# Decode attention: the row maxima one unit later, the heads' sums over four units, and another sharing of the last batch's value halves

## The reference

```python
def fox_sample(q, k_new, v_new, logf_new, k_past, v_past, logf_past):
    ...
    c = jnp.cumsum(lf_all, axis=1).transpose(0, 2, 1)
    s = jnp.einsum('bqhd,bkhd->bhqk', q, k_all, preferred_element_type=F32) * FOX_SCALE
    s = s + cq[..., :, None] - c[:, :, None, :]
    s = jnp.where(kpos[None, :] <= qpos[:, None], s, -jnp.inf)
    p = jax.nn.softmax(s, axis=-1).astype(v_all.dtype)
    return jnp.einsum('bhqk,bkhd->bqhd', p, v_all)
```

## Time and profile before

| | |
|---|---|
| median of 3 runs | 2482.54 us (2477.68 to 2482.71) |
| the profiled execution | 2480.07 us |
| its span, first to last instruction | 2478.2 us |
| TensorE, VectorE, ScalarE, GpSimd busy | 91%, 38%, 37%, 26% of the span |
| mean granted TensorE clock | 0.951 |

### The profile page before, as it was taken

The page is one execution under the profiler, slowest core; times in us unless marked ns, Lnnn a source line. Parts: engine busy times, 40 slices in busy tenths (PEclk is TensorE's granted clock), DMA queues, the critical chain, the costliest instruction groups (busy, mean ns, idle before and its releaser), DMA issues. The chain is left out here.

```text
span 2478.2 us, 31007 instructions
## 1 busy us (share of the span) xinstructions
PE 2255.6 (91%) x11248; PEld 1820.7 (73%) x11248; DVE 951.0 (38%) x1497; ACT 924.6 (37%) x1455; POOL 648.1 (26%) x390
## 2 busy tenths in 40 slices
PE   6999999889999788999997499699999999995999
PEld 5999999767777566666765278577777888874687
DVE  3334444353663757777776200410021321111000
ACT  4233333223443435777777210422234333333100
POOL 1231121220220001555545542021122111113420
PEclk9999999889999888999998699799999999997999
DMA  6122232201200307899996453432222322214431
GB/s 155 29 54 53 49 82 56 56 23 46 61 14 30 97 1 264 306 319 316 313 312 224 134 153 108 152 105 77 72 92 84 111 71 71 71 37 150 146 102 53
DMA packets 258377, 288.06 MB, mean 116 GB/s; under 512 B 70538, under 2 KB 169740, under 8 KB 258124
## 3 DMA queue, kind: packets, MB, share of 16 engines
q1 hardware_dynamic: 240986, 252.84, 33.0%
q10 hardware_dynamic: 17266, 33.59, 3.7%
HBM read 246.09 MB, written 41.32 MB: 116 GB/s over the span
## 5 line engine op out<-in xcount | busy, mean ns | idle before, releaser
L226 PE MATMUL bank<-whi,x_hi 128*128 128x512 f32 (+1 forms) x1536 | 592.9, 386 | 20.1 <-POOL wlo L206 14.9
L228 PE MATMUL bank<-wlo,x_hi 128*128 128x512 f32 (+1 forms) x1536 | 580.1, 378 | 0.0
L230 PE MATMUL bank<-whi,x_lo 128*128 128x512 f32 (+1 forms) x1536 | 579.5, 377 | 0.0
L226 PEld LDWEIGHTS bank<-whi,x_hi 128*128 128x128 f32 x1536 | 293.0, 191 | 81.9 <-POOL wlo L206 19.4
L230 PEld LDWEIGHTS bank<-whi,x_lo 128*128 128x128 f32 x1536 | 293.1, 191 | 41.6
L259 ACT ACTIVATE projected<-bank 128x512 f32<-128x512 f32 (+1 forms) x160 | 92.1, 576 | 620.6 <-PE bank L230 591.7
L228 PEld LDWEIGHTS bank<-wlo,x_hi 128*128 128x128 f32 x1536 | 293.8, 191 | 39.3 <-issue 0.7
L2069 POOL TENSOR_TENSOR dec_v_lo<-dec_v,dec_v_hi 128x1024 fp32r<-128x1024 f32 x96 | 237.2, 2492 | 220.0 <-ACT dec_v_hi L2417 220.0
L206 POOL TENSOR_TENSOR wlo<-wraw,whi 128x512 fp32r<-128x512 f32 (+1 forms) x192 | 230.5, 1233 | 32.6 <-ACT whi L199 32.6
L2236 DVE TENSOR_TENSOR dec_kt_lo<-bank,dec_kt_hi 128x512 fp32r<-128x512 f32 x256 | 170.4, 684 | 100.6 <-ACT dec_kt_hi L2407 100.2
L2407 ACT ACTIVATE dec_kt_hi<-bank 128x512 fp32r<-128x512 f32 x256 | 150.5, 596 | 107.5 <-PE bank L2096 96.3
(11 more groups left out here) (335 smaller groups left out, 3306.2 us busy)
## 6 DMA issues: line engine op xcount, KB each, us to landing
dec_k<-cache_k SPq DMA_DIRECT2D x256, 256.0 KB, 4.0
dec_v<-cache_v SPq DMA_DIRECT2D x256, 256.0 KB, 4.4
wraw<-w_in_even SPq DMA_DIRECT2D x32, 512.0 KB, 6.4
wraw<-w_in_odd SPq DMA_DIRECT2D x16, 1024.0 KB, 8.5
gv<-projected ACTq DMA_DIRECT2D x4, 2304.0 KB, 8.1
gm_v<-gv SPq DMA_DIRECT2D x8, 1152.0 KB, 6.0
m<-gm_mt ACTq DMA_DIRECT2D x8, 1056.0 KB, 4.1
wraw<-w_in_odd SPq DMA_DIRECT2D x4, 2048.0 KB, 8.8
```

Source lines behind the costliest of these rows:

```text
L226: pe.matmul(bank[:, 0:width], e.xhi[:, k, c:c + P], e.whi[:, k, 0:width], start=(k == 0), stop=False)
L228: pe.matmul(bank[:, 0:width], e.xhi[:, k, c:c + P], e.wlo[:, k, 0:width], start=False, stop=False)
L230: mm = pe.matmul(bank[:, 0:width], e.xlo[:, k, c:c + P], e.whi[:, k, 0:width], start=False, stop=(k == KD - 1))
```

## The change

The row maxima move from unit 36 to 37 of the batch, behind the key split of 36. `heads` is cut in four: the pick of the heads at unit 70 (38 of the next batch), the two sums at 71 and 72, the adding and scaling at 73 (41), each behind its unit's key split. The store of the result goes with `HEADS_AT + 2` from 70 to 75. In the last batch the odd value pieces go to VectorE and the even ones to GpSimd, eight each, where it was four and twelve. `by_vector` and `by_pool`, which count the pieces for the waits, take the batch as well, and SP, GpSimd and TensorE call them with it. The shorter loop bound of TensorE only drops units in which it has nothing to do.

```diff
-HEADS_AT = VALUE_AT[-1] + 2
+MAXES_AT = LOW[-1] + 1
+PICK_AT = VALUE_AT[-1] + 4
+HEADS_AT = PICK_AT + 3
-def on_vector(p):
-    return p % 4 == 3
+def on_vector(r, p):
+    return p % 4 == 3 if r < DB - 1 else p % 2 == 1
...
-                for u in range(UNITS * (DB - 1) + HEADS_AT):
+                for u in range(UNITS * (DB - 1) + VALUE_AT[-1] + 1):
...
-                def heads(r):
-                    s = Chain(steps_t, r)
+                def pick_heads(r):
+                    step_t[0] = Chain(steps_t, r)
                     dve.wait_ge(out_written.sem, out_written.at(r, 2))
                     dve.tensor_tensor(picked_o[:], outb[0:2 * rows, :].rearrange("p (h d) -> p h d", h=H),
                                       own_head[:].unsqueeze(2).broadcast_to([2 * rows, H, HD]), ALU.mult).then_inc(
                         out_read.sem, 1)
+
+                def sum_heads(r, dst, src):
+                    s = step_t[0]
                     dve.wait_ge(out_read.sem, out_read.at(r, 2))
-                    dve.tensor_reduce(o_hi[:], picked_o[0:rows].rearrange("p h d -> p d h"), AX, ALU.add).then_inc(
+                    dve.tensor_reduce(dst[:], picked_o[src].rearrange("p h d -> p d h"), AX, ALU.add).then_inc(
                         s.sem, s.one())
-                    dve.tensor_reduce(o_lo[:], picked_o[rows:2 * rows].rearrange("p h d -> p d h"), AX,
-                                      ALU.add).then_inc(s.sem, s.one())
+
+                def heads(r):
+                    s = step_t[0]
                     dve.wait_ge(s.sem, s.reached())
                     dve.tensor_tensor(o_hi[:], o_hi[:], o_lo[:], ALU.add).then_inc(s.sem, s.one())
...
                             store_scores(r, x)
-                            if x == GROUPS // 2 - 1:
-                                maxes(r)
+                    if rounds_at(u, MAXES_AT) is not None:
+                        maxes(rounds_at(u, MAXES_AT))
                     if n < DB * GROUPS:
                         split_keys(n // GROUPS, n % GROUPS, j)
...
                     for r, p in pieces_at(u, LEAD - 1):
-                        if on_vector(p):
+                        if on_vector(r, p):
                             split_values(r, p)
+                    if rounds_at(u, PICK_AT) is not None:
+                        pick_heads(rounds_at(u, PICK_AT))
+                    if rounds_at(u, PICK_AT + 1) is not None:
+                        sum_heads(rounds_at(u, PICK_AT + 1), o_hi, slice(0, rows))
+                    if rounds_at(u, PICK_AT + 2) is not None:
+                        sum_heads(rounds_at(u, PICK_AT + 2), o_lo, slice(rows, 2 * rows))
                     if rounds_at(u, HEADS_AT) is not None:
                         heads(rounds_at(u, HEADS_AT))
```

More of the change, by code:

```diff
@@ L1840, with by_vector, by_pool @@
 VALUE_AT = [FIRST_VALUE + 3 * p // 2 for p in range(VPIECES)]
-HEADS_AT = VALUE_AT[-1] + 2
-def on_vector(p):
-    return p % 4 == 3
[L1849 to L1856, removed]
+MAXES_AT = LOW[-1] + 1
[3 more added lines that the diff above has]
+    return p % 4 == 3 if r < DB - 1 else p % 2 == 1
+def by_vector(r, p):
+    return sum(on_vector(r, q) for q in range(p + 1))
+def by_pool(r, p):
+    return p + 1 - by_vector(r, p)
 def rounds_at(u, at):
@@ L1979, in attention_block @@
         v_hi_ready = c.begin("v_hi_ready", VPIECES)
-        v_lo_vector = c.begin("v_lo_vector_ready", by_vector(VPIECES - 1))
-        v_lo_pool = c.begin("v_lo_pool_ready", by_pool(VPIECES - 1))
+        v_lo_vector = c.begin("v_lo_vector_ready", by_vector(0, VPIECES - 1))
+        v_lo_pool = c.begin("v_lo_pool_ready", by_pool(0, VPIECES - 1))
         v_used = c.begin("v_pieces_used", VPIECES)
@@ L2037, in load_values @@
                         r, p = (n - RING) // GROUPS, 2 * ((n - RING) % GROUPS) + 1
[L2038 to L2041, removed]
+                        if on_vector(r, p) or on_vector(r, p - 1):
+                            sp.wait_ge(v_lo_vector.sem, v_lo_vector.at(r, by_vector(r, p)))
+                        if not on_vector(r, p) or not on_vector(r, p - 1):
+                            sp.wait_ge(v_lo_pool.sem, v_lo_pool.at(r, by_pool(r, p)))
                     for j, page in pages_of(n):
@@ L2084, in _ @@
                     for p in range(VPIECES):
-                        if not on_vector(p):
+                        if not on_vector(r, p):
                             split_values(r, p)
@@ L2147, in values @@
                         pe.wait_ge(out_read.sem, out_read.at(r, 1))
-                    if on_vector(p):
-                        pe.wait_ge(v_lo_vector.sem, v_lo_vector.at(r, by_vector(p)))
+                    if on_vector(r, p):
+                        pe.wait_ge(v_lo_vector.sem, v_lo_vector.at(r, by_vector(r, p)))
                     else:
-                        pe.wait_ge(v_lo_pool.sem, v_lo_pool.at(r, by_pool(p)))
+                        pe.wait_ge(v_lo_pool.sem, v_lo_pool.at(r, by_pool(r, p)))
                     slot = (VPIECES * r + p) % VRING
@@ L2327, in heads @@
                     s.end()
-                step = [None]
+                step, step_t = [None], [None]
                 def first(dve):
```

## The result

The median of four runs is 2502.97 us (2501.83 to 2505.23), against 2481.89 before (four runs, 2477.68 to 2482.71): a ratio of 1.009, 95% interval 1.0072 to 1.0107, or some 21 us slower. That was the direction forecast, at about twice the forecast size of 10.5. The profiled execution took 2505.23.

What follows compares the result with a forecast made beforehand. TensorE was taken to bound the kernel, busy 47.26 of 51 us. Six boundaries +16.8, first boundary +0.6, last batch -5.5 gave +11.9 us: 2492 to 2494.4 by basis, said as 2493, range 2476 to 2508.

Steps and rivals of the forecast that it cites:

- The walk up to the small sum: VectorE at a middle boundary: exponentials at 3.14 us after the store, small sum due at 10.32, held by GpSimd to 12.02.
- the scaling: VectorE operation after the small sum: taken as not held by GpSimd; the two small operations together take 0.42 us.
- held twice: Rival at the six boundaries: GpSimd holds small sum and scaling, 3.6 + 1.6 us each, +26.3, 2506; chance 0.21.
- 6 x (1.20 + 1.6): Six boundaries with heads: first value product 1.20 us later, plus 1.6 of half clock each; 16.8 us.
- the sum of 11.9: Whole kernel: net slowdown of 11.9 us from middle boundaries, first boundary and last batch.
- TensorE's wait: Middle boundary: waits of 2.7 and 1.01 us become one piece ahead of the transposition, 8.6 to 13.80, 5.2 us.
- The half clock: TensorE after its long wait: half clock falls on the value products, 1.6 us a boundary, bounds 0.41 and 1.6.
- The later maxima: Batch boundary: a key split of 0.62 us ahead of the row maxima delays the exponentials, 2.52 to 3.14.
- ScalarE's wait: Store of the heads, moved from unit 38 to 43: its 1.7 us wait goes, unless heads end after 12.8.
- The last batch: Eight and eight halves: GpSimd takes 26.2 us plus 3.3 of gaps; closing pair at 1385.3 against 1390.86, gain 5.5.
- The bound: Decode stage: TensorE sets the pace; under 4 us of holes a batch is all that reordering VectorE can win.

Runs made afterwards that it cites:

- pool_waits: Changed kernel, but GpSimd starts a batch's first value half only after the previous batch's scaling is done: 2478.10 us, ratio 0.9996.
- heads_late: Changed kernel with adding, scaling and store three units later, in unit 44 behind the split of the probabilities: 2478.35 us, ratio 0.9996.
- maxes_back: Changed kernel with the row maxima back in unit 36: 2497.65 us, ratio 1.0071.
- scale_scalar: Changed kernel with the scaling made by ScalarE right ahead of the store, the adding still on VectorE: 2489.67 us, ratio 1.0044.
- value_later: Changed kernel with maxima in unit 36, adding and scaling in 44, new tokens' transposition and value products two units later: 2439.46 us, ratio 0.9836.
- value_later_whole: Kernel before with eight and eight last-batch halves, value products and the whole heads behind them two units later: 2441.24 us, ratio 0.9847.
- tail_only: Kernel before with only the last batch's value halves shared eight and eight: 2472.03 us, ratio 0.9968.
- value_later3: Like value_later, but new tokens' transposition and value products three units later instead of two: 2448.05 us, ratio 0.9873.

## Why the prediction was right in its sign and half in its size

**The walk up to the small sum was right.** Exponentials forecast at 3.14 and found at 3.09; the split behind them 6.33 and 6.28; GpSimd's first half 7.32 and 7.28; the second sum's end 9.70 and 9.60; the small sum due at 10.32, found at 10.24 and held to 12.02, as forecast. (The row that the hold was taken from the earlier trace rows is the square of one SBUF tensor and not a sum of two, as the prediction has it; the hold was the same.)

**The step that failed is the scaling.** The prediction held the small sum once and took the scaling as not held, because its form, at 396 ns for 256 columns, showed no sign of the faster form. It took 2.25 us, six times in six. What the rival *held twice* said happened: GpSimd's third half, already waiting, went first. The rate in the earlier trace rows was no guide: in pool_waits the same operation takes 0.24 us in the same place without GpSimd, no faster than the small sum's 0.20, and yet it is held. And the hold needs a GpSimd half that follows at once; where none did, in the last batch, the scaling took 0.24. The Trainium skill (SBUF — State Buffer, Who interferes with whom) says that tensor_scalar is among the operations that can be blocked for a whole GpSimd instruction, and that reductions on this chip never are; by that rule the time would have been 2506, and the trace agrees with both parts (2.25 us; the two sums at 1.06 and 1.02, which were 1.07 and 1.00 before).

In the sum it is the term 6 x (1.20 + 1.6): probabilities at 14.83, not 13.06, so +1.77 at each boundary. With the forecast 2.80 that makes 4.57 of the 4.63 measured. Over six boundaries it is 10.6 us; the last batch took 1.2 of it back, which leaves 9.4 of the 9.8 by which the sum of 11.9 fell short of 21.7.

**TensorE's wait moved, as forecast,** into one piece ahead of the transposition: 7.40 us, from 8.16 to 15.56: the forecast 5.2, the 1.77 above, and 0.44 because TensorE was through before the forecast 8.6. Its wait for key halves went; in the first batch, with no heads, the step was +0.58 against 0.6.

**The half clock was sized right, but lies elsewhere.** From the transposition to the value product 2.35 us instead of 1.32, and from there to the next store 40.17 instead of 39.51: 1.69 a boundary, where 1.6 was taken. The prediction put all of it behind the first value product; 0.66 is there, and 1.03 lies in the 1.32 ahead of it that the walk kept as before. So the agreement is in part luck: in heads_late the same two stretches lose 1.03 and 1.2. heads_late shows that it comes with the single wait and not with the holds.

**The later maxima were sized wrong, without harm to the sum.** Their 0.57 stands within the 1.20, but taking them back returns nothing: in maxes_back the value product comes 0.55 earlier, and the stretch from it to the next store is 0.54 longer (40.71 against 40.17). So the parts of a boundary can't be priced one by one here.

**ScalarE's wait was not gone** but moved from the store of unit 38 to that of 43, 1.8 us each. The prediction named the condition (heads that end after 12.8) and they ended at 14.3. Whether this wait costs anything by itself was not tried; in scale_scalar, where it is 2.3 us in all instead of 10.8, the period gained 1.83, which is not more than the hold's 2.25.

**The last batch** gave 6.7 instead of 5.5. The gaps between GpSimd's halves were 5.8 us, not 3.3, but its eight halves took 21.9, not 26.2: the forecast let each of VectorE's eight splits hold GpSimd for 0.93, and at 2.33 a half alone they held it 3.3 us in all.

**The bound held:** the holes of under 4 us in a batch are what value_later took out, 3.75 a period, though by moving TensorE's work and not by reordering VectorE's.

## What to carry to other kernels

Before a small VectorE operation is moved, look at what GpSimd does at its new time: two operations of 0.45 us together cost 4 us there, and the same two cost nothing three units later or with GpSimd standing still. Where the form of an operation is among those that may be held, a bare rate from another place is no reason to count it as free; look for a row of the same form beside a running GpSimd instruction, and without one give the hold the larger chance. And where the engine that sets the pace waits for a chain, ask first whether it has other work to do in the meantime: reordering the chain lost 21 us, and moving its consumer two units later won some 30 (value_later_whole against tail_only).

## What the runs showed of the hardware

- Between two VectorE operations 0.04 us apart, a GpSimd instruction that was waiting for its turn got in, so that both were held, one after the other, to the ends of two GpSimd instructions (1101.57 and 1103.86 against 1101.48 and 1103.81, worked out). Where no GpSimd instruction followed at once, the second one took its 0.24 us (the changed kernel's last batch, and value_later3).
- The hold goes by the end of the GpSimd instruction, not by the size of the VectorE operation: 32 x 64 elements took 0.36, 1.46, 1.78 or 2.35 us, by the moment at which they met it.
- After a wait TensorE took up its work 0.55 us earlier in one kernel than in another, and the full clock came back later, 19.9 against 19.4 us after the store (worked out from granted clocks of 0.55 and 0.81), so the earlier start bought nothing.
- In the kernel with the value products two units later and the scaling held, waits of the same length (2.68 us) were followed by the half clock at every second boundary only: the periods alternate between 53.8 and 52.2 us (granted clock 0.53 and 1.00 between 17.6 and 21.1 us after the stores at 1130.81 and 1078.59).
